# A ring of eight row slots instead of ten, and a second kept weight block

## What is computed

```
q = (xt @ w_query).reshape(T, PEER_HEADS, 2, QUERY_HALF)
s = jnp.einsum('thpd,hpnd->thpn', q, sub_keys)
s_top, i_top = lax.top_k(s, PEER_TOPK)            # 16 best of 128 keys in each half
g_s, sel = lax.top_k(cand, PEER_TOPK)             # 16 best of the 256 sums
u = jnp.take(expert_u, ic, axis=0)                # 8 heads x 16 experts = 128 rows a token
a = jnp.einsum('td,thkd->thk', xc, u)
w = gc * jax.nn.gelu(a)
y = jnp.einsum('thk,thkd->td', w, jnp.take(expert_v, ic, axis=0))
```

## Time and profile before

| | |
|---|---|
| device time, median of 3 runs | 2409.63 us (2407.55 to 2409.93) |
| profiled execution, device time | 2408.89 us |
| its span | 2407.1 us |
| TensorE busy | 1816.8 us, 75% |
| VectorE busy | 1695.2 us, 70% |
| ScalarE / GpSimd busy | 765.5 us, 32% / 958.9 us, 40% |
| bytes moved by DMA | 967.95 MB, mean 402 GB/s |
| mean granted TensorE clock | 0.89 |

### The profile page before, as it was taken

One profiled execution on the slowest core, in us unless ns is written; L12 is line 12 of the kernel. 1 busy time (PEld: TensorE's weight loads), 2 busy tenths in 40 slices (PEclk: granted clock), 3 DMA queues, 4 the chain that ended last, 5 costly groups with the idle time before them and its releaser, 6 DMA issues.

```text
span 2407.1 us, 19433 instructions
## 1 busy us (share of the span) xinstructions
PE 1816.8 (75%) x5886; PEld 945.6 (39%) x5886; DVE 1695.2 (70%) x3577; ACT 765.5 (32%) x2232; POOL 958.9 (40%) x772
## 2 busy tenths in 40 slices
PE   7867777877788778896767867977777788876555
PEld 3642333633545335563323333642333435422111
DVE  3388876688656887657876575588766855987776
ACT  2123553234113242122322462233325512432222
POOL 0034544434422354323554344324533533455552
PEclk9889888989989899898888998988889989988787
DMA  5399999999999999999999999999999999999996
GB/s 193 146 379 421 421 421 422 423 416 421 422 422 422 398 418 421 423 423 421 407 421 423 424 417 422 422 418 409 417 425 413 418 424 421 397 421 422 421 422 287
DMA packets 127832, 967.95 MB, mean 402 GB/s; under 512 B 14960, under 2 KB 15088, under 8 KB 20336
## 3 DMA queue, kind: packets, MB, share of 16 engines
q0 software_dynamic: 110592, 805.36, 80.7%
q1 hardware_dynamic: 17136, 161.36, 16.2%
HBM read 965.61 MB, written 1.05 MB: 402 GB/s over the span
## 4 chain that ended last, share of the span: by engine, by line
DMA 56%; PE 18%; DVE 12%; issue 5%; ACT 4%; POOL 4%; SPq 0%; ACTq 0%; DVEq 0%; POOLq 0%
DMA ring<-in_uv,idx 56%; PE y L1101 10%; DVE ring L1474 5%; POOL ring L903 4%; PE acc L944 3%; DVE x L1465 2%; PE acc L955 2%; PE y L944 1%; ACT diag L1272 1%; PE tp L1030 1%; ACT wgt L1262 1%; ACT L1259 1%; DMA wbuf<-in_wts 0%; ACT ge L1259 0%; PE acc L1071 0%
## 5 line engine op out<-in xcount | busy, mean ns | idle before, releaser
L1101 PE MATMUL y<-ring,diag 128*128 128x512 f32 x2124 | 1162.1, 693 | 514.3 <-ACT diag L1272 502.4
L903 POOL DMA_INDIRECT ring<-in_uv,idx x768 | 958.7, 1248 | 1417.2 <-PE y L1101 811.3
L1474 DVE CUSTOM_DVE_ANT_0 ring<-ring,h 128x1024 f32<-128x1024 f32 x768 | 927.7, 1221 | 443.5 <-DMA ring<-in_uv,idx 439.1
L1101 PEld LDWEIGHTS y<-ring,diag 128*128 128x128 f32 x2124 | 434.7, 217 | 1138.5 <-ACT diag L1272 678.7
L1259 ACT ACTIVATE ge<-a 128x2 f32<-128x2 f32 x384 | 78.0, 203 | 1343.2 <-DVE a L1474 1339.4
L1465 DVE SCALAR_TENSOR_TENSOR x<-ring,wgt,x 128x1024 f32<-128x1024 f32 x237 | 303.8, 1282 | 99.9 <-ACT wgt L1262 91.4
L955 PEld LDWEIGHTS acc<-fT,wbuf 128*128 128x128 f32 x2176 | 261.3, 198 | 39.9 <-issue 39.6
L955 PE MATMUL acc<-fT,wbuf 128*128 128x128 f32 x2176 | 263.8, 281 | 13.2 <-issue 8.8
L944 PE MATMUL acc<-wbuf,fT 128*128 128x512 f32 (+2 forms) x536 | 240.6, 601 | 5.6 <-DMA wbuf<-in_wts 3.0
L1272 ACT ACTIVATE diag<-id_s,wgt 128x128 f32<-128x128 f32 x531 | 195.3, 397 | 12.0
L1262 ACT ACTIVATE wgt<-ge,gate 128x1 f32<-128x1 f32 x768 | 184.2, 287 | 12.6
(11 more groups left out here) (144 smaller groups left out, 962.4 us busy)
## 6 DMA issues: line engine op xcount, KB each, us to landing
wbuf<-in_wts SPq DMA_DIRECT2D x64, 2048.0 KB
ring<-in_uv,idx POOLq DMA_INDIRECT x768
caches<-in_wts SPq DMA_DIRECT2D x3, 2048.0 KB, 9.8
kbuf<-in_keys SPq DMA_DIRECT2D x24, 256.0 KB
gain<-in_gains SPq DMA_DIRECT2D x11, 512.0 KB
wbuf<-in_wts SPq DMA_DIRECT2D x2, 1664.0 KB
wbuf<-in_wts SPq DMA_DIRECT2D x2, 1280.0 KB
x<-in_x SPq DMA_DIRECT2D x2, 512.0 KB, 11.6
```

Source lines behind the costliest of these rows:

```text
L903: nc.gpsimd.indirect_dma_start(ring[:, n % RING, :], None, uv[layer(s)], bass.IndirectOffsetOnAxis(ap=idx[:, tile(s), k:k + 1], axis=0),). ...
L1101: mm = nc.tensor.matmul(y[half][:], diag[:, (d - 1) % DIAGS, :], ring[:, n % RING, D + half * BLK:D + (half + 1) * BLK], start=(k == y_end ...
L1474: ins = v.tensor_tensor_reduce(u, u, h[:, tile(s), :], 1.0, 0.0, ALU.mult, ALU.add, a[:, c:c + 1])
```

## The change

`RING` goes from 10 to 8. The 16 KB that this frees on each partition become `kept1`, a second place for kept blocks. `KEPT` becomes a list of two lists, one for each place; the first is the one of before. The second place holds (0, out1), then (1, u0), then (2, q). Each of these three blocks is now loaded once, in the order of `LOADS` of the first tile, and used by both. It has a semaphore of its own. A kept block waits for the second tile's last product with the block that it replaces; the first of each place waits for nothing. Three loads leave `LOADED` for good, and the blocks after them go into the other half of `wbuf` and wait for other products than before. In the planner, `lean` is now also 4 us once no dense TensorE work is left. Rows still come in pairs.

```
-RING = 10
+RING = 8
-KEPT = [(0, "qkv0"), (0, "out0"), (1, "c0")]
+KEPT = [[(0, "qkv0"), (0, "out0"), (1, "c0")], [(0, "out1"), (1, "u0"), (2, "q")]]
+def kept_place(l, name):
+    for i, held in enumerate(KEPT):
+        if (l, name) in held:
+            return i, held.index((l, name))
+    return None
...
-            lean = LEAN if waits and waits < at + NEAR else 0.0
+            lean = LEAN if waits and waits < at + NEAR or not dense_of["PE"] else 0.0
...
+        kept1 = sb("kept1", [P, WBLK])
...
-        kept = caches[:, 1040:1040 + WBLK]
+        kept = [caches[:, 1040:1040 + WBLK], kept1[:]]
...
-                    j = KEPT.index((layer(s), name))
+                    i, j = kept_place(layer(s), name)
                     if j:
-                        l2, name2 = KEPT[j - 1]
+                        l2, name2 = KEPT[i][j - 1]
                         sp.wait_ge(acc_done.sem, acc_done.count(TILES * l2 + 1, name2))
-                    sp.dma_start(kept[:], wts[W_BASE[layer(s)] + names.index(name)]).then_inc(kept_in, 16)
+                    sp.dma_start(kept[i], wts[W_BASE[layer(s)] + names.index(name)]).then_inc(kept_in[i], 16)
```

More of the change, by code:

```diff
@@ L313, in loads @@
         for name, _ in W_BLOCKS[layer(s)]:
-            if (layer(s), name) in KEPT:
+            if kept_place(layer(s), name):
                 if tile(s) == 0:
@@ L752, in build @@
         w_in = [sem("w_in0"), sem("w_in1")]
-        kept_in = sem("kept_in")
+        kept_in = [sem(f"kept_in{i}") for i in range(len(KEPT))]
         k_in = [sem("k_in0"), sem("k_in1")]
@@ L933, in weights @@
                 if n is None:
-                    pe.wait_ge(kept_in, 16 * (KEPT.index((layer(s), name)) + 1))
-                    return kept[:]
+                    i, j = kept_place(layer(s), name)
+                    pe.wait_ge(kept_in[i], 16 * (j + 1))
+                    return kept[i]
                 pe.wait_ge(w_in[n % 2], 16 * (n // 2 + 1))
```

## The result

The changed kernel takes 2414.14 us (median of 14 runs, 2411.85 to 2418.21), the one before 2409.44 in the same comparison: ratio 1.0023, 95% interval 1.0015 to 1.0031. It is slower by 4.7 us, where I had forecast 5.4 faster. The time lies in the range of 2395 to 2420, but on the wrong side of no change.

A forecast was written before the change was run, and what follows sets the result against it. The prediction took DMA bandwidth to bound the kernel from 130 us on. Loads -14.9, depth +7.0 and tail's end +2.3 summed to -5.6 us, giving 2404.0 us; the 8-in-10 range was 2395 to 2420.

The forecast's parts named there:

- The bound: From 130 us on the kernel runs at DMA speed, most slices moving 421 to 424 GB/s; the opening does not.
- The loads: Three second weight loads dropped from the DMA-saturated part, all counting in full: 3 x 4.97 = 14.9 us saved.
- the fourth rival: Only two loads count, the third falling into time the opening left idle: 2409.0 us, chance 0.05.
- The depth: Two gather slots fewer cost nothing in quiet stretches and 1.4 us at each of five dips, 7.0 us.
- a turn that still fits into 19.9 us: Eight gather slots must turn over in 19.9 us; a quiet turn took 17.9, leaving 2.0 us to spare.
- the dips: Five 20 us windows at 353 to 397 GB/s, most at a step's top-k, losing 12.1 us together before the change.
- What moves: the tail: Last step: nearly all slots go to TensorE, hidden behind the DMA; only the very end costs 2.3 us.
- The tail's end: Last pair, both on TensorE: one more 1.98 us product and some 0.3 us of ScalarE in line, 2.3 us.
- The depth is free: Rival: lagging engines and shorter weight traffic cover the dips, so two fewer slots cost nothing: 2397.0 us, chance 0.2.
- Eight slots are too few in the top-k stretches: Slower rival: each of the five dips costs two full slots of wire, 24.9 us: 2421.9 us, chance 0.2.
- My sign for this rival: The five dip windows reading under 320 GB/s, with new ones elsewhere, instead of 330 to 370, would show it right.
- The tail becomes bound by TensorE: Rival: at the lower clock, 46% of the 40 pairs after 2200 cost 2.0 us more each: +37, 2441, chance 0.05.

The follow-up runs named there:

- run 1: Kernel before, ring of ten and its own order, second loads of (0, out1), (1, u0), (2, q) cut to 16 columns each: 2395.32 us, ratio 0.9942.
- run 3: Kernel before with RING = 8 but the planner still counting ten slots, so the old order and loads stay: 2418.47 us, ratio 1.0039.
- run 5: Changed kernel with each engine keeping the order planned for ten slots and old loads, old tail rule included: 2400.67 us, ratio 0.9961.
- run 6: Kernel before with ten slots in hardware but the order the planner makes for eight: 2427.05 us, ratio 1.0072.
- run 2: Kernel before with RING = 8 and nothing else, same loads, order planned anew for eight: 2436.96 us, ratio 1.0109.
- run 4: Changed kernel with the planner's 0.5 us handicap against dense work dropped for step 5's dense operations: 2403.18 us, ratio 0.9973 to the kernel before.
- run 7: Changed kernel without its rule for the tail (lean as before): 2412.5 us, ratio 1.0014 to the kernel before.
- run 11: Changed kernel without the tail rule and without the planner's handicap against dense work in step 5: 2404.83 us, ratio 0.998 to the kernel before.

## Why the prediction was wrong, step by step

**The bound** was read rightly: 14.6 us for three loads without anything else (run 1), against 14.9.

**The loads** all counted, also the first at the edge of the opening, so the fourth rival is out. The count I gave, 65 blocks to `wbuf`, was wrong: 58 full blocks and the four shorter ones make 62, and three go to `kept`. The first loads had left `wbuf` as well; the bytes are the same.

**The depth** was sized at 7.0 us and measured 8.6 alone (run 3), and 4.9 with the loads gone (14.6 less the 9.7 of run 5); the intervals do not tell the two apart, and 7.0 fits both. The reading behind it held too: quiet stretches at 421 with eight slots, a turn that still fits into 19.9 us, thin losses at the dips.

**The step that failed is "What moves: the tail".** There I looked at the one line of the planner that the diff changes, and priced the rest of the order at nothing, without a word. But `RING` and `KEPT` are inputs of the planner. With eight slots it wrote another list for every engine, and the dense part of step 5 slipped behind ten to fourteen more row slots. That costs 16.7 us with ten slots in place (run 6) and 18.5 with eight (runs 2 and 3). In the changed kernel it is 4.7 + 9.7 = 14.4 us against run 5, which differs in the order alone (the rule for the tail is part of it), or 4.7 + 14.6 - 8.6 = 10.7 by the parts; dense work first in step 5 gives back 11.0 (run 4). With the order held fixed, the sum of the prediction without its tail, -14.9 + 7.0 = -7.9, stands beside -9.7 (run 5).

**The tail's end.** From the last dot to the output's issue it is 10.2 us before and 11.9 after, +1.7 for the 2.3 that I gave:

```profile
2399.23 1.23 DVE L1484 CUSTOM_DVE_ANT_0 ring<-ring,h 128x1024 f32<-128x1024 f32 x1 [1.22 <-DMA ring<-in_uv,idx]
...
2401.70 3.70 PE L1111 MATMUL y<-ring,diag 128*128 128x512 f32 x8 [1.24 <-ACT diag L1282]
...
2411.12 0.34 SPq L900 DMA_DIRECT2D out<-h  x1
```

It is real in the trace and lost in the medians (runs 7 and 11). Issue to landing became 13.4 us, not 12.4. The adds fell by 26, to 211, not by 40.

**The rivals.** "The depth is free" is refuted by run 3. "Eight slots are too few in the top-k stretches" came near the time but by another mechanism: the deepest dip is no top-k stretch short of slots but a wait for an index with all slots free, and it stays with ten slots (run 6). My sign for this rival, windows under 320 GB/s, came up (267 and 124) and would have pointed at the wrong cause: it asked how deep a dip is, not what GpSimd waits for in it. I had one sentence there on late rows holding back dense work; it is the other way round, late dense work held back the rows. "The tail becomes bound by TensorE" is refuted: the clock there is 1.00.

**What stays open.** Why the planner lets the dense part slip just between the two attentions of step 5. The 7.3 us of the window at 1824, where GpSimd waited up to 19 us for slots on VectorE,

```profile
1801.84 1.93 POOL L912 DMA_INDIRECT ring<-in_uv,idx  x1 [19.18 <-DVE x L1475]
...
1836.91 1.14 POOL L912 DMA_INDIRECT ring<-in_uv,idx  x1 [13.00 <-PE y L1111]
```

goes away with the old order (in run 5 the stretch from 1800 to 1900 reads 422 GB/s), so it is a matter of the order as well, but it was not tried apart. And whether the 3.7 us by which run 5 beats its parts, and the 3.4 us between the order's 14.4 and the 11.0 of run 4, are more than noise.

## What to carry to other kernels

When a size is an input of a planner, the change is two changes: the resource and a new order. Compare the order lists before you price anything, and run the new resource with the old order, which here cost 8.6 us against 27.1. A bound by bandwidth still has a second clock beside it: who says what to fetch next. Look at each point where a stream must know an index, and write down how far the index is ahead (here 4 us); every saving in bytes brings the stream to that point earlier, and is only worth something if the index comes along. And before you explain a single dip, look whether another run with the same order up to that point shows it too; here two such executions differed by 4 to 6 us in one slice.

## What the runs showed of the hardware

TensorE did twice the row slots in the tail for 28% more busy time. Between 2250 and 2350 it was 20 slots, 57.4 us busy at a granted clock of 0.77; after the change it is 40 slots, 73.7 us at 1.00. The stretch with one slot on TensorE in each 5 us had been granted 1.2 GHz for part of the time, and the one with two ran at 2.4 throughout. The DMA paces both, 422 and 421 GB/s, so it bought no time.
